# Routing on unweighed rows, with the norm vector folded into the routing matrices

## The reference, cut to what matters

```
xn = rms_norm(h, norm_ffn[l])            # h * rsqrt(mean(h*h) + eps) * g
lg = xn @ w_group + b_group              # 4 columns
le = xn @ w_expert + b_expert            # 16 columns, masked to the best group
top2 of le -> experts, softmax weights
y  = sum over experts of gate * (silu(xn @ w1[e]) * (xn @ w3[e])) @ w2[e]
h  = h + y
```

## Time and profile before

| | |
|---|---|
| median of 3 runs | 1046.54 us (1043.63 to 1046.66) |
| profiled execution | 1048.5 us, its span 1046.4 us |
| TensorE busy | 993.8 us (95%), 4978 instructions |
| VectorE busy | 758.9 us (73%) |
| ScalarE busy | 606.7 us (58%) |
| GpSimd busy | 84.9 us (8%) |
| mean granted TensorE clock | 0.977 |
| chain that ended last | TensorE 75%, VectorE 11%, DMA 7%, ScalarE 4%, issue 2% |

### The profile page before, as it was taken

The page is one execution under the profiler, slowest core; times in us unless marked ns, Lnnn a source line. Parts: engine busy times, 40 slices in busy tenths (PEclk is TensorE's granted clock), DMA queues, the critical chain, the costliest instruction groups (busy, mean ns, idle before and its releaser), DMA issues.

```text
span 1046.4 us, 12942 instructions
## 1 busy us (share of the span) xinstructions
PE 993.8 (95%) x4978; PEld 727.8 (70%) x4978; DVE 758.9 (73%) x700; ACT 606.7 (58%) x506; POOL 84.9 (8%) x110
## 2 busy tenths in 40 slices
PE   5999999999999999999999998979998989999997
PEld 5889998879665666666655645866885757766664
DVE  5446656176699888888859483564658999988996
ACT  5436432234577787777744335343457878887880
POOL 4100000002200000000003030000030000000013
PEclk9999999998999999999999999899899989999999
DMA  9642622682899999999775030106389999999975
GB/s 329 196 171 93 221 81 92 238 354 120 296 366 382 397 387 396 391 396 386 318 243 199 3 122 10 72 1 257 145 310 366 385 388 385 390 397 412 413 325 181
DMA packets 54762, 277.70 MB, mean 265 GB/s; under 512 B 6400, under 2 KB 8864, under 8 KB 45872
## 3 DMA queue, kind: packets, MB, share of 16 engines
q1 hardware_dynamic: 43520, 240.21, 59.6%
q0 software_dynamic: 8736, 28.51, 8.1%
q10 hardware_dynamic: 2464, 8.39, 2.0%
HBM read 259.21 MB, written 18.04 MB: 265 GB/s over the span
## 4 chain that ended last, share of the span: by engine, by line
PE 75%; DVE 11%; DMA 7%; ACT 4%; issue 2%; ACTq 0%; SPq 0%; POOL 0%; DVEq 0%
PE ps L187 20%; PE ps L193 10%; PE ps L530 4%; PE ps L584 4%; PE ps L1393 4%; DMA raw<-in_moe_w_dram 4%; PE ps L1390 4%; PE ps L627 3%; DVE raw_lo L1112 3%; PE ps L2203 3%; PE ps L590 2%; PE ps L538 2%; PE ps L1425 2%; ACT moe_wh L1107 2%; PE ps L634 2%
## 5 line engine op out<-in xcount | busy, mean ns | idle before, releaser
L1112 DVE TENSOR_TENSOR raw_lo<-raw,moe_wh 128x4096 fp32r<-128x4096 f32 x48 | 212.0, 4423 | 36.3 <-ACT moe_wh L1107 36.2
L1112 DVE TENSOR_TENSOR moe_wl<-moe_raw,moe_wh 128x4096 fp32r<-128x4096 f32 x48 | 212.0, 4423 | 33.1 <-ACT moe_wh L1107 33.0
L1107 ACT ACTIVATE moe_wh<-raw 128x4096 fp32r<-128x4096 f32 x48 | 174.5, 3635 | 18.4 <-DMA raw<-in_moe_w_dram 9.5
L1107 ACT ACTIVATE moe_wh<-moe_raw 128x4096 fp32r<-128x4096 f32 x48 | 173.9, 3625 | 11.6 <-DMA moe_raw<-in_moe_w_dram 11.6
L187 PE MATMUL ps<-moe_wh,moe_x 128*72 128x512 f32 x512 | 124.3, 395 | 1.7 <-DVE moe_x L1258 1.5
L330 DVE TENSOR_TENSOR raw_lo<-raw,gm_wh 128x4096 fp32r<-128x4096 f32 x12 | 53.1, 4425 | 70.9 <-ACT gm_wh L324 70.4
L187 PEld LDWEIGHTS ps<-moe_wh,moe_x 128*72 128x72 f32 x512 | 71.0, 142 | 45.2 <-DVE moe_x L1258 2.6
L187 PE MATMUL ps<-moe_wh,moe_hTh 128*72 128x512 f32 (+1 forms) x256 | 82.1, 402 | 4.6 <-DVE moe_hTl L1263 2.8
L187 PE MATMUL ps<-moe_wh,moe_hTl 128*72 128x512 f32 (+1 forms) x256 | 80.7, 396 | 0.0
L324 ACT ACTIVATE gm_wh<-raw 128x4096 fp32r<-128x4096 f32 x11 | 40.0, 3634 | 60.5 <-DMA raw<-in_gm_w_in_dram 31.0
L1390 PE MATMUL ps<-moe_wh,moe_x 128*128 128x512 f32 x224 | 62.3, 420 | 10.2 <-DVE moe_x L1258 10.2
(11 more groups left out here) (415 smaller groups left out, 1701.0 us busy)
## 6 DMA issues: line engine op xcount, KB each, us to landing
raw<-in_moe_w_dram SPq DMA_DIRECT2D x48, 2048.0 KB, 11.7
moe_raw<-in_moe_w_dram SPq DMA_DIRECT2D x48, 2048.0 KB, 12.2
raw<-in_gm_w_in_dram SPq DMA_DIRECT2D x7, 2048.0 KB, 7.8
raw<-in_gm_w_out_dram SPq DMA_DIRECT2D x4, 2048.0 KB, 7.5
moe_yrows<-moe_rows ACTq DMA_DIRECT2D x16, 288.0 KB
moe_rows<-moe_xrows POOLq DMA_DIRECT2D x14, 288.0 KB, 9.4
moe_rows<-moe_xrows POOLq DMA_DIRECT2D x14, 256.0 KB, 8.9
moe_yrows<-moe_rows ACTq DMA_DIRECT2D x14, 256.0 KB
```

Of the source, the lines that this page charges most:

```text
L1107: nc.scalar.activation(w_hi[hi][:], w_raw[slot], ACT.Copy).then_inc(wh_ready, 1)
L1112: nc.vector.tensor_tensor(w_lo[slot], w_raw[slot], w_hi[hi][:].bitcast(F32), ALU.subtract).then_inc(wl_ready, 1)
```

## The change

The transposes read `h` itself, by slices with a step of eight elements, and wait for `h_mixed`. The norm vector is multiplied once, in layer 0, into both layers' routing matrices (it is loaded into `g_in`, and GpSimd reloads `g_in` with the attention's vectors afterwards, ahead of the load of `gain`). `weigh_rows` stays, for the expert products, but only tile 0 is weighed between the residual sums; tiles 1 and 2 come after all three sums. The scaling of `rows` by the inverse root goes from VectorE to ScalarE, after the root. TensorE's order becomes transposes(0), transposes(1), logits(0), logits(1), transposes(2), logits(2). GpSimd's scatter and TensorE's first gather also wait for ScalarE's scaling.

```
 gm_pool:
-            g.dma_start(g_in[:, 0:KD], A["kv_norm"]...).then_inc(ld_route, 16)
-            g.dma_start(g_in[:, KD:2 * KD], A["norm_mix"][1]...).then_inc(ld_route, 16)
-            g.dma_start(g_in[:, 2 * KD:], A["q_a_norm"][0]...).then_inc(ld_route, 16)
+            for l in range(2):
+                g.dma_start(g_in[:, l * KD:(l + 1) * KD], A["norm_ffn"][l]...).then_inc(ld_route, 16)
 gm_vector:
+            v.wait_ge(ld_route, 16 * 10)
+            w_by_k = wroute[:].rearrange("p l k n -> p (l k) n")
+            nc.vector.tensor_tensor(w_by_k, w_by_k, g_in[:, 0:2 * KD].unsqueeze(2).to_broadcast([P, 2 * KD, NT]), ALU.mult
+                                    ).then_inc(rt_xn, 1)
             moe_split_l(v, 0, 0, 0, 0)
...
-                weigh_rows(v, 0, t)
+                if t == 0:
+                    weigh_rows(v, 0, 0)
+            weigh_rows(v, 0, 1)
+            weigh_rows(v, 0, 2)
 moe_pool:
                 g.dma_start(xrows[SLOTS:ROWS], ...).then_inc(pad_written, 16)
+                g.wait_ge(rt_xn, 1)
+                g.dma_start(g_in[:, 0:KD], A["kv_norm"]...).then_inc(ld_route, 16)
+                g.dma_start(g_in[:, KD:2 * KD], A["norm_mix"][1]...).then_inc(ld_route, 16)
+                g.dma_start(g_in[:, 2 * KD:], A["q_a_norm"][0]...).then_inc(ld_route, 16)
                 g.wait_ge(gm_xn, 2 * TILES)
             g.dma_start(gain[:], A["norm_ffn"][l:l + 1, :].partition_broadcast(P)).then_inc(ld_gain, 16)
             g.wait_ge(rt_dst, l + 1)
+            g.wait_ge(rt_xTc, 2 * TILES * (l + 1))
 route_vector:
-            inverse_of_roots(v)
-            for t in range(TILES):
-                v.wait_ge(rt_xT, TILES * l + t + 1)
-                dve_link(v, nc.vector.tensor_scalar(rows[:, t], rows[:, t], stat[:, 1, t:t + 1], None, ALU.mult))
-            v.wait_ge(ld_route, 16 * 11)
+            roots["rms"] += 1
+            v.wait_ge(rms_ready, roots["rms"])
+            nc.vector.reciprocal(stat[:, 1, 0:TILES], stat[:, 1, 0:TILES]).then_inc(rt_xn, 1)
+            v.wait_ge(rt_xn, 4 * l + 5)
 route_scalar, after the root:
+            a.wait_ge(rt_xn, 4 * l + 5)
+            for t in range(TILES):
+                nc.scalar.activation(rows[:, t], rows[:, t], ACT.Copy, scale=stat[:, 1, t:t + 1]).then_inc(rt_xTc, 1)
 route_tensor:
-            if l == 0:
-                pe.wait_ge(ld_route, 16 * 11)
+            pe.wait_ge(rt_xn, 1)
             def transpose_rows(t):
-                pe.wait_ge(rt_xn, TILES * l + t + 1)
+                pe.wait_ge(h_mixed, TILES * l + t + 1)
...
-                                               rows[:, t, k * P:(k + 1) * P], ident)
+                                               by_slice(h[:, t], KD)[:, k], ident)
             logits(0)
+            logits(1)
             transpose_rows(2)
-            logits(1)
             logits(2)
 moe_tensor:
+            pe.wait_ge(rt_xTc, 2 * TILES * (l + 1))
             gather_x(0)
```

More of the change, by code:

```diff
@@ L300, in gm_pool @@
                 g.dma_start(broute[:, l, NG:], A["moe_b_expert"][l:l + 1, :].partition_broadcast(P)).then_inc(ld_route, 16)
-            g.dma_start(g_in[:, 0:KD], A["kv_norm"].rearrange("(p k) -> p k", k=KD)).then_inc(ld_route, 16)
-            g.dma_start(g_in[:, KD:2 * KD], A["norm_mix"][1].rearrange("(p k) -> p k", k=KD)).then_inc(ld_route, 16)
-            g.dma_start(g_in[:, 2 * KD:], A["q_a_norm"][0].rearrange("(p k) -> p k", k=3)).then_inc(ld_route, 16)
+            for l in range(2):
+                g.dma_start(g_in[:, l * KD:(l + 1) * KD], A["norm_ffn"][l].rearrange("(p k) -> p k", k=KD)).then_inc(ld_route, 16)
             for m in range(2, N_V):
@@ L870, in moe_pool @@
                 g.dma_start(xrows[SLOTS:ROWS], A["x_prompt"][0, 0:CAP, :]).then_inc(pad_written, 16)
+                g.wait_ge(rt_xn, 1)
+                g.dma_start(g_in[:, 0:KD], A["kv_norm"].rearrange("(p k) -> p k", k=KD)).then_inc(ld_route, 16)
+                g.dma_start(g_in[:, KD:2 * KD], A["norm_mix"][1].rearrange("(p k) -> p k", k=KD)).then_inc(ld_route, 16)
+                g.dma_start(g_in[:, 2 * KD:], A["q_a_norm"][0].rearrange("(p k) -> p k", k=3)).then_inc(ld_route, 16)
                 g.wait_ge(gm_xn, 2 * TILES)
@@ L1059, in route_tensor @@
         def route_tensor(pe, l):
-            if l == 0:
-                pe.wait_ge(ld_route, 16 * 11)
+            pe.wait_ge(rt_xn, 1)
             def transpose_rows(t):
-                pe.wait_ge(rt_xn, TILES * l + t + 1)
+                pe.wait_ge(h_mixed, TILES * l + t + 1)
                 for k in range(KD):
                     last = nc.tensor.transpose(ps[:, ROW_BANK[l][t] + k // 4, (k % 4) * P:(k % 4 + 1) * P],
-                                               rows[:, t, k * P:(k + 1) * P], ident)
+                                               by_slice(h[:, t], KD)[:, k], ident)
                 last.then_inc(rt_xT, 1)
             def logits(t):
-                pe.wait_ge(rt_xTc, TILES * l + t + 1)
+                pe.wait_ge(rt_xTc, 2 * TILES * l + t + 1)
                 for k in range(KD):
@@ L1712, in at_vector @@
             v.wait_ge(ld_rows, 32)
+            v.wait_ge(ld_route, 16 * 13)
             nc.vector.tensor_tensor(w_dq, w_dq, g_in[:, KD:2 * KD].unsqueeze(2).to_broadcast([P, KD, QR]), ALU.mult
@@ L1791, in at_vector @@
                                         ps[:, O_BANK[t]:O_BANK[t] + 2], ALU.add).then_inc(h_mixed, 1)
-                weigh_rows(v, 1, t)
+                if t == 0:
+                    weigh_rows(v, 1, 0)
+            weigh_rows(v, 1, 1)
+            weigh_rows(v, 1, 2)
         def latent_rows(v, t, cos3, sin3):
```

## The result

The changed kernel takes 1051.17 us (median of 20 runs, 1047.72 to 1055.45), the kernel before 1047.36 (20 runs beside them). The ratio is 1.0036, its 95% interval 1.002 to 1.0052: +3.8 us, between +2.1 and +5.4. The forecast was 1047.4, with a range from 1044.6 to 1049.8.

What follows compares the result with a forecast made beforehand. The prediction took TensorE's routing chain and its granted clock as the bound. Layer 0's +0.9 us and layer 1's 0, all else hidden, moved the median from 1046.54 to 1047.4 us, range 1044.6 to 1049.8.

Steps and rivals of the forecast that it cites:

- Order of the logits, layer 0, "with the fall at 236.8": Layer 0's routing: with the clock falling at 236.8, logits end at 243.5 instead of 242.28, +1.2 us.
- through the fillers: Forty filler matmuls behind the logits pass layer 0's delay on as +0.6 to +1.2 us, taken as +0.9; layer 1 0.
- the clock recovers later: Rival, slower, chance 0.06: all layer 0 fillers at the lower clock, early fall in layer 1; +4.0 us, 1050.5.
- The hole costs its 1.1 us: Both routings: TensorE stands idle 1.1 us between transposes(2) and logits(2), as nothing covers ScalarE's copy.
- Layer 1, 0: Layer 1's routing: earlier start and uncovered copy cancel, logits end 0.2 us earlier, taken as 0; up to +0.5.
- Transposes at the lower level 1.6: Eight transposes(2) in layer 0's routing take 1.6 us at the lower clock, against 0.92 at the upper.
- Scaling on ScalarE, 3.3, hidden: Routing: three scaled copies on ScalarE take 3.3 us, the exponential ends about 254 in layer 0; cost 0.
- Folding 0.4, hidden: One VectorE instruction multiplying in the norm vector takes about 0.4 us before the first expert half's wait; cost 0.
- Strided reads 0: Transposes reading every eighth element of h cost 0; 48 ns in each of 48 would make 2.3 us.
- Gain load, landing by 229.1, 0: Layer 0's norm vector, issued near 216.5, lands between 220.3 and 229.1; no cost until 229.7.
- The clock stays up: Rival, faster, chance 0.08: upper clock through both routings, 6.8 us gained, 1039.7; in one layer alone about 1043.
- The gain load comes late: Rival, slower, chance 0.07: late norm vector blocks weighing(0) and transposes(1); landing after 18 us costs 4.8 us, 1052.2.

Runs made afterwards that it cites:

- the first profile: First profiled execution of the changed kernel against the kernel before: 1047.79 us with a span of 1046.1, near the shortest of its 20 runs.
- its near variants: Changed kernel with the scalings of rows back on VectorE, 1.0027, and with layer 0's norm vector loaded early again, 1.0039, both against the kernel before.
- 4 and 8 of them: Changed kernel, new logits order, with 4 fillers behind transposes(1) and 8 behind transposes(2): 1.0008 against the kernel before.

## Why the prediction was wrong

The hole, its place and its length were right, and the size of layer 0's term was not; about 2 of the 3.8 us the routings don't hold at all. That the first profile agreed with the sum to a tenth was luck: its clock fell when it had fallen in the kernel before. Point by point:

- *Order of the logits, layer 0, "with the fall at 236.8".* This is the step that failed. The sum took the clock's fall and return from one execution, and "through the fillers" made "the middle, +0.9" of it. Executions with a like fall gave just that. But the fall comes at another moment in each (4.8 to 8.1 us behind the last wide matmul), and the mean over the profiles is +1.9 us for this term (21.4 against 19.5), with routings of 22.2 and 22.3 us where it came early. The rival "the clock recovers later" got 0.06 and priced forty fillers at the lower level; no profile has that (7.4 us for forty was the longest in these seven, not 9.3). What does happen is a long low stretch from an early fall, in three of seven, and it belonged in the mean.
- *The hole costs its 1.1 us.* It does, and more. With fillers behind transposes(2) in both orders (in the old one with four more behind transposes(1)), the new order takes 18.3 and 18.5 us and the old one 17.3 to 17.6: the hole keeps a cost of about 0.9 us a layer. That the loss still goes (0.9996) is because the fillers win back more at the clock than that, as the profiles have it.
- *Layer 1, 0.* Right for the whole change: 20.6 against 20.8. Within it the earlier start gains 0.8 (20.0 with the old order) and the new order gives back 0.6.
- *Transposes at the lower level 1.6.* Measured 1.72. *Scaling on ScalarE, 3.3, hidden:* 3.23, hidden; the exponential started at 252.8 and held nobody. *Folding 0.4, hidden:* 0.48, at 213.67 in idle time. *Strided reads 0:* sixteen transposes took 1.95 us, before 1.91. The penalty that the Trainium skill, SBUF — State Buffer, Door 1, lets one expect for steps beyond 16 bytes is again hardly seen: 0.04 us in sixteen, where 48 ns in each would be 0.77.
- *Gain load, landing by 229.1, 0:* it landed at 227.0, 11 us behind its issue, and moving it back changed nothing that can be measured.
- *The clock stays up* did not happen in the changed kernel; its lever is real, though, as the fillers show. *The gain load comes late* did not cost.

The routings account for +1.9 - 0.2 = +1.7 us. The runs say +3.8, with 2.1 the lower end. Layer 0's experts took 311.6 to 312.6 us with the new order and 311.1 to 311.7 with the old where the clock held, and 313.0 to 314.0 wherever it fell again between 272 and 281, in profiles of either order. Attention varied from 172.0 to 177.3 and layer 1's experts from 288.3 to 296.5. Over the eleven profiles of the table the spans differ by 5.4 us in the mean, of which layer 0's routing is 1.9, its experts 0.9, attention 1.0 and layer 1's experts 1.6; with such spreads that is a hint at where the missing 2 us lie, and no more.

That the order of the logits carries the loss is shown by the runs: the changed kernel with the old order at 0.9998 and 1.0005 in two measurements, four measurements of the changed one and its near variants at 1.0027 to 1.0039, and the order alone at 1.0057. That the clock is the lever is shown by the six fillers, which compute nothing and let logits(2) start no earlier. How the order costs 3.8 us and not 0.9 is shown for about half.

## What to carry to other kernels

Where a stretch of narrow TensorE work lies between wide ones, a hole of 1 us costs its own time and what goes with it at the clock: sum the stage for several moments at which the clock can fall, not for the one in the profile at hand. Before moving work to fill a hole, try a few dummy matmuls in it; and before moving work off an engine, see whether it is hidden only because something else takes long. One profile of a kernel whose runs spread by 0.7% is one draw; its place among the runs belongs beside each sum made from it.

## What the runs showed of the hardware

In layer 0's routing the stretches at the lower clock lasted about 3.4, 6.8, 10.2 or 13.7 us, with nothing in between, in every kernel in which the clock fell there. With six fillers of 256 columns in the hole, 1.28 us at the lower level, the stretch lasted 3.4 us in both layers, and the clock was back during logits(2). With six transposes of 128 columns it did so in one layer and not in the other. And fillers can fail: with 4 and 8 of them the clock that had fallen at 234.7 stayed low for 13.7 us. A stretch of 3.4 us also came once without any (kernel before with 52 fillers at the end, layer 0), after a fall at 238.1.
